# Gate matrices of an expert layer: from one-hot products on TensorE to indirect DMAs that add into DRAM, and one rounding moved from VectorE to ScalarE

## What is computed

```python
def one_block(xb):                                   # 128 tokens
    q = (xb @ w_query).reshape(PEER_BLOCK, PEER_HEADS, 2, PEER_HALF)
    s = jnp.einsum("thpd,hpkd->thpk", q, sub_keys)   # 8 heads, 2 halves, 128 keys
    s1, i1 = lax.top_k(s[:, :, 0], 16)
    s2, i2 = lax.top_k(s[:, :, 1], 16)
    cand = s1[..., :, None] + s2[..., None, :]
    sc, flat = lax.top_k(cand.reshape(..., 256), 16)
    e = i1[flat // 16] * 128 + i2[flat % 16]         # expert numbers
    g = jax.nn.softmax(sc, axis=-1)
    a = jax.nn.gelu(jnp.einsum("thkd,td->thk", u_emb[e], xb))
    return jnp.einsum("thk,thkd->td", g * a, v_emb[e])
```

## Time and profile before

| what | value |
|---|---|
| median of three runs | 3485.08 us (3483.61 to 3486.14) |
| span of the profiled execution | 3486.2 us |
| instructions | 47,324 |
| up stage, layer 0 / layer 1 | from 611.2 / from 2188.0 us, 746 us each |
| down stage, layer 0 / layer 1 | about 1357 to 1900 / 2934 to 3469 us |
| moved by DMA | 735 MB, 211 GB/s on average |

### The profile page before, as it was taken

The page is one execution under the profiler, slowest core; times in us unless marked ns, Lnnn a source line. Parts: engine busy times, 40 slices in busy tenths (PEclk is TensorE's granted clock), DMA queues, the critical chain, the costliest instruction groups (busy, mean ns, idle before and its releaser), DMA issues.

```text
span 3486.2 us, 47324 instructions
## 1 busy us (share of the span) xinstructions
PE 3400.2 (98%) x18196; PEld 2951.7 (85%) x18196; DVE 2360.2 (68%) x4309; ACT 1221.5 (35%) x1635; POOL 1194.6 (34%) x746
## 2 busy tenths in 40 slices
PE   7999889999999999999999989999999999999998
PEld 3886578888888889999999768888888888999998
DVE  6777720994487724998997330895477723999997
ACT  3216633333455532222223333333355532222222
POOL 0000033454100002776772453454200002877761
PEclk9999989999999999999999999999999999999999
DMA  7771030344455556999995230344455555999995
GB/s 284 260 252 49 25 145 1 127 145 145 160 191 222 198 180 219 365 359 366 384 376 210 73 122 12 110 146 145 159 206 186 222 183 202 357 370 361 359 361 198
DMA packets 286132, 735.16 MB, mean 211 GB/s; under 512 B 33362, under 2 KB 116947, under 8 KB 266196
## 3 DMA queue, kind: packets, MB, share of 16 engines
q1 hardware_dynamic: 203988, 530.63, 43.1%
q0 software_dynamic: 45056, 134.38, 10.3%
q10 hardware_dynamic: 36864, 67.13, 5.0%
HBM read 612.48 MB, written 119.54 MB: 210 GB/s over the span
## 4 chain that ended last, share of the span: by engine, by line
PE 93%; POOL 2%; DVE 2%; DMA 1%; ACT 1%; issue 1%; SPq 0%; DVEq 0%; POOLq 0%; ACTq 0%
PE ps L1373 40%; PE ps L1411 28%; PE ps L1175 5%; PE ps L1326 5%; PE ps L1277 5%; PE ps L1386 3%; PE ps L1203 2%; PE ps L1235 1%; POOL picked L1496 1%; PE ps L1215 1%; PE ps L1318 1%; PE ps L1129 1%; PE ps L1089 0%; POOL ring_lo L1484 0%; DMA modall<-in_w_mod 0%
## 5 line engine op out<-in xcount | busy, mean ns | idle before, releaser
L1373 PE MATMUL ps<-xhi,Uhi 128*128 128x512 f32 x2048 | 807.5, 394 | 0.0
L1373 PE MATMUL ps<-xhi,Ulo 128*128 128x512 f32 x2048 | 798.4, 390 | 0.0
L1373 PE MATMUL ps<-xlo,Uhi 128*128 128x512 f32 x2048 | 796.6, 389 | 0.0
L1496 POOL DMA_INDIRECT picked<-act_scratch,aidx x256 | 381.9, 1492 | 985.0 <-DMA act_scratch<-act_st 907.6
L1411 PE MATMUL ps<-Hhi,Vhi 128*128 128x384 f32 x2048 | 687.3, 336 | 6.7 <-DVE Hlo L2003 6.7
L1411 PE MATMUL ps<-Hlo,Vhi 128*128 128x384 f32 x2048 | 685.9, 335 | 0.0
L1411 PE MATMUL ps<-Hhi,Vlo 128*128 128x384 f32 x2048 | 685.8, 335 | 0.0
L1027 ACT CAST Vhi<-Vraw 128x1024 fp32r<-128x1024 f32 x256 | 269.8, 1054 | 787.0 <-PE ps L1411 766.4
L986 ACT ACTIVATE act_st<-ps 128x512 f32<-128x512 f32 x256 | 153.1, 598 | 869.6 <-PE ps L1373 535.1
L1373 PEld LDWEIGHTS ps<-xhi,Ulo 128*128 128x128 f32 x2048 | 384.3, 188 | 82.2
L1373 PEld LDWEIGHTS ps<-xlo,Uhi 128*128 128x128 f32 x2048 | 384.9, 188 | 77.6
(11 more groups left out here) (283 smaller groups left out, 4547.1 us busy)
## 6 DMA issues: line engine op xcount, KB each, us to landing
Uraw<-in_UT SPq DMA_DIRECT2D x128, 1024.0 KB, 5.7
Vraw<-in_V SPq DMA_DIRECT2D x256, 512.0 KB, 5.7
act_scratch<-act_st ACTq DMA_DIRECT2D x256, 256.0 KB, 5.5
G_scratch<-G_st SPq DMA_DIRECT2D x24, 2048.0 KB, 8.2
act<-act_scratch SPq DMA_DIRECT2D x256, 192.0 KB, 6.0
Gin<-G_scratch SPq DMA_DIRECT2D x192, 256.0 KB
modw<-in_w_mod SPq DMA_DIRECT2D x80, 512.0 KB, 4.8
ring<-in_query SPq DMA_DIRECT2D x8, 2048.0 KB, 8.0
```

The lines of the kernel that those rows point to most:

```text
L1373: mm = nc.tensor.matmul(up_bank(m), w, x[:, k, :], start=(k == 0 and j == 0), stop=(k == KT - 1 and j == 2))
L1496: nc.gpsimd.indirect_dma_start(picked[:, :, :].rearrange("p h k -> p (h k)")[:, p:p + 1], None, act_dram[layer].rearrange("m p (t o) -> (m ...
```

## The change

In place of the transposes, one-hot matrices, products, evictions and stores of G, POOL adds the weights one by one into a G in DRAM that was zeroed before: for each of the 384 pairs (token tile r = 1 to 3, head, place k) an indirect DMA of 128 floats with 128 offsets and `compute_op=ALU.add`. The offsets are computed at the end of `picks`. `PUTS` gives the order of the 24 groups of 16; a group waits until the group before of the same token tile has landed, since heads can hit the same element. G is now laid out as a tile of experts by 384 tokens, and the down stage loads it tile by tile, 192 KB each, four ahead.

The zeroes are written by SP from a zeroed strip in SBUF: 16 DMAs of 1.5 MB for layer 0 behind the second bias table, 16 for layer 1 beside tiles 41 to 71 of layer 0's up stage. POOL's subtractions end at tile 12; DVE does those of tiles 13 to 54 between the steps of `picks` (14 points for each of the token tiles that come second to fourth) and the rest behind them. The token tiles are routed in the order 1, 2, 3, 0. In the down stage ACT rounds H, ahead of the rounding of V two tiles on, where DVE did. The third `gate_in` chunk is loaded right behind the first two.

```diff
...
-HOTS_AT = 56
-REST_AT = HOTS_AT + 1
-EXP_AT = {13: 0, 25: 1, 37: 2, 49: 3}
-TURN_AT = {40: 1, 51: 2, 53: 3}
+ROUTE = (1, 2, 3, 0)
+REST_AT = 13
+POINTS = 14
+EXP_AT = {11: 0, 26: 1, 40: 2, 54: 3}
+WEIGHTS_AT = 56
+PUTS = ((0, 0), (0, 1), (0, 2), (1, 0), (0, 3), (1, 1), (0, 4), (2, 0), (1, 2), (0, 5), (2, 1), (1, 3),
+        (0, 6), (2, 2), (1, 4), (0, 7), (2, 3), (1, 5), (2, 4), (1, 6), (2, 5), (1, 7), (2, 6), (2, 7))
+NZ = 3 * P // 2
+ZROWS = 16
+ZERO_AT = 40
+NZERO = NE * TD // (P * ZROWS * NZ)
 LEAD = 112
 NPK = PH * TOPK
...
-        G_dram = nc.dram_tensor("G_scratch", (DEPTH, NCHT, P, NKEY, CHT), F32, kind="Internal").ap()
+        G_dram = [nc.dram_tensor(f"G_scratch{layer}", (NT, P, TD), F32, kind="Internal").ap()
+                  for layer in range(DEPTH)]
...
                 load_chunk(n)
+            def zero_gates(layer, n):
+                flat = G_dram[layer].rearrange("m p t -> (m p t)").rearrange("(p n z) -> p n z", p=P, z=NZ)
+                sp.dma_start(flat[:, n * ZROWS:(n + 1) * ZROWS, :],
+                             zeros[:, :].unsqueeze(1).to_broadcast([P, ZROWS, NZ])).then_inc(G_zeroed, 16)
...
                     sp.wait_ge(bias_used, h - 1)
                 sp.dma_start(btab[h % 2][:, :, :, :], a["btab"][2 * h:2 * h + 2].rearrange("h p s k -> p h s k")
                              ).then_inc(bias_in[h % 2], 16)
+                if h == 1:
+                    sp.wait_ge(zeros_ready, 1)
+                    for n in range(NZERO):
+                        zero_gates(0, n)
...
-            def load_gates(layer, q, c0, c1):
-                if q >= 2:
-                    sp.wait_ge(H_ready, layer * NT + (q - 1) * NGRP)
-                elif q == 1:
+            def load_gates(layer, m):
+                if m >= 4:
+                    sp.wait_ge(H_ready, layer * NT + m - 3)
+                elif m >= 2:
                     sp.wait_ge(up_mm, (layer + 1) * NT)
-                sp.dma_start(Gin[q % 2][:, c0:c1, :, :],
-                             G_dram[layer, c0:c1, :, q * NGRP:(q + 1) * NGRP, :].rearrange("c p j t -> p c j t")
-                             ).then_inc(G_in[q % 2], 16)
+                sp.dma_start(Gin[m % 4][:, :], G_dram[layer][m]).then_inc(G_in[m % 4], 16)
...
                     if m % 2 == 0 and 2 <= m < NT - 4:
                         load_U(m // 2 + 2)
-                    if m >= 1:
-                        for b in batches_after(m - 1):
-                            if (b + 1) * TOK % CHT == 0:
-                                store_gates(b * TOK // CHT)
+                    if layer == 0 and ZERO_AT <= m < ZERO_AT + 2 * NZERO and m % 2 == 1:
+                        zero_gates(1, (m - ZERO_AT) // 2)
                     if m == LEAD:
                         load_V(layer, 0)
                         load_V(layer, 1)
                         load_act(layer, 0)
-                for n in range(2):
-                    sp.wait_ge(G_stored[n], 16 * (layer + 1) * NCHT // 2)
-                for c in range(0, NCHT, GPIECE):
-                    load_gates(layer, 0, c, c + GPIECE)
+                for r in range(1, TT):
+                    sp.wait_ge(G_put[r], 16 * NPK * (layer + 1))
+                load_gates(layer, 0)
+                load_gates(layer, 1)
...
+                load_gates(layer, 2)
+                load_gates(layer, 3)
...
                         load_V(layer, m + NVRAW)
                     if m + 4 < NT:
                         load_act(layer, m + 4)
-                    if m % NGRP < NCHT // GPIECE and m // NGRP + 1 < NT // NGRP:
-                        c = m % NGRP * GPIECE
-                        load_gates(layer, m // NGRP + 1, c, c + GPIECE)
-                    if layer == 0 and 64 <= m < 64 + RING - 1:
+                        load_gates(layer, m + 4)
+                    if layer == 0 and 64 <= m < 64 + RING:
                         load_chunk(W_GIN + m - 64)
-                    if layer == 0 and m == NT - 4:
-                        sp.wait_ge(H_ready, NT - NGRP)
-                        load_chunk(W_GIN + RING - 1)
...
+            def round_H(layer, m):
+                act_e.wait_ge(H_step, layer * NT + m + 1)
+                if m >= 3:
+                    act_e.wait_ge(dn_mm, layer * (NT - 1) + m - 2)
+                nc.scalar.copy(Hhi[m % 3][:, :], Hf[m % 2][:, :]).then_inc(H_hi, 1)
             def peer_dense(layer):
                 for m in range(NT):
-                    i = layer * NT + m
+                    round_H(layer, m)
                     if m + 2 < NT:
                         split_V(layer, m + 2)
...
                 for m in range(NT):
                     up(m)
-                    if m in TURN_AT:
-                        turn_picks(TURN_AT[m])
-                    for b in batches_after(m):
-                        gate_weights(b)
...
                                             ALU.subtract).then_inc(U_split, 1)
+            def put_gates(layer):
+                pool.wait_ge(G_zeroed, 16 * NZERO * (layer + 1))
+                for order, h in PUTS:
+                    r = ROUTE[order]
+                    if h == 0:
+                        pool.wait_ge(pick_ready, layer * TT + order + 1)
+                    at_least(pool, G_put[r], 16 * (layer * NPK + h * TOPK))
+                    for k in range(TOPK):
+                        nc.gpsimd.indirect_dma_start(
+                            G_dram[layer].rearrange("m p (t o) -> (m p t) o", o=1),
+                            bass.IndirectOffsetOnAxis(ap=gidx[r][:, h * TOPK + k:h * TOPK + k + 1], axis=0),
+                            pick[r][:, 3, h, k:k + 1], None, compute_op=ALU.add).then_inc(G_put[r], 16)
...
             peer_rests(0)
+            put_gates(0)
             peer_rows(0)
...
+                def picks(order):
+                    r = ROUTE[order]
                     chosen = pick[r]
+                    def between(point):
+                        if order >= 1 and point is not None:
+                            rest_of_U(REST_AT + (order - 1) * POINTS + point)
...
                         for i in rows:
                             last = nc.vector.max_index(ids(i)[:, 8:16], vals(i)[:, 8:16], src(i))
                         step(last)
+                        between(points[4])
                     top16(range(HP), lambda i: topv[:, i // 2, i % 2, :], lambda i: topi[:, i // 2, i % 2, :],
-                          lambda i: S[:, i, r, :])
+                          lambda i: S[:, i, r, :], (0, 1, 2, 3, 4))
+                    if order >= 1:
+                        weights(order - 1)
...
                     step(last)
+                    between(5)
...
-                          lambda i: cand[:, 0, i, :])
+                          lambda i: cand[:, 0, i, :], (None, 6, None, 7, 8))
...
                     step(nc.vector.tensor_tensor(rank[:, 1, :, :], candi[:, :, :], rank[:, 1, :, :], ALU.subtract))
+                    between(9)
...
                     for half, keys in enumerate((key1[:, :, :], chosen[:, 2, :, :])):
                                                      ALU.is_equal))
                         step(nc.vector.tensor_tensor(eq[:, :, :, :], eq[:, :, :, :],
                                                      topi[:, :, half, :].unsqueeze(2).to_broadcast(shape), ALU.mult))
+                        between(10 + 2 * half)
                         step(nc.vector.tensor_reduce(keys, eq[:, :, :, :], AX, ALU.add))
+                        between(11 + 2 * half)
                     nc.vector.tensor_tensor(chosen[:, 3, :, :], candv[:, :, :],
...
+                    step(nc.vector.scalar_tensor_tensor(out=key1[:, :, :], in0=key1[:, :, :], scalar=float(NKEY),
+                                                        in1=chosen[:, 2, :, :], op0=ALU.mult, op1=ALU.add))
+                    if r > 0:
+                        nc.vector.tensor_scalar(gidx[r][:, :].rearrange("p (h k) -> p h k", h=PH), key1[:, :, :],
+                                                float(TD), row_no[:, r - 1:r], ALU.mult, ALU.add)
...
+                for r in range(1, TT - 1):
+                    if layer == 0:
+                        nc.vector.tensor_scalar(row_no[:, r:r + 1], row_no[:, 0:1], float(r * P), None, ALU.add)
+                for order in range(TT):
+                    picks(order)
+                for m in range(REST_AT + (TT - 1) * POINTS, NT):
+                    if m == WEIGHTS_AT:
+                        weights(TT - 1)
                     rest_of_U(m)
...
                 def gated(m):
-                    i = layer * NT + m
-                    q = m // NGRP
                     dve.wait_ge(act_in[m % 4], 16 * (layer * NT // 4 + m // 4 + 1))
-                    dve.wait_ge(G_in[q % 2], 16 * (NCHT // GPIECE) * (layer * NT // NGRP // 2 + q // 2 + 1))
-                    nc.vector.tensor_tensor(Hf[m % 2][:, :].rearrange("p (c t) -> p c t", t=CHT),
```

(11 more changed lines are left out.)

196 lines of the change are left out of this document (31 added, 165 removed).

## The result

The change makes the kernel slower: 3714.8 us (3700.4 to 3716.6), 1.0652 times the time before, 95% interval 1.0632 to 1.0673. The profiled execution spans 3711.7 us where that of before spans 3486.2. The forecast was 3393, and its range ended at 3620.

What follows compares the result with a forecast made beforehand. The prediction took PE's instruction stream, busy 98% of the span, as the bound. From a span of 3486.2 us it took 99 saved, plus 2 and 5, giving 3394.2, on the median 3393; own range 3375 to 3420, with rivals up to 3620.

Steps and rivals of the forecast that it cites:

- What leaves PE: Up stage: without gate matmuls and transposes it takes 696.7 us instead of 746.1, saving 49.5 us a layer, 99 in all.
- (d): Layer 1's zeroing beside tiles 41 to 71 of layer 0: gelu waits for stores, 0 to 6 us, taken as 2.
- The start and the collisions: POOL, up stage: puts start near 696; waiting for DVE instructions adds 0.24 us a put during routing, 0.11 after.
- The price of a put: POOL, up stage: a put costs 0.94 us like a gather, plus gap and collisions, so puts end at 1257, hidden.
- c: Mean cost of a put with its gap: forecast 1.39 us; PE waits beyond 1.526, and the sign turns at 1.63.
- puts dearer than gathers: Rival, POOL in the up stage: at 1.79 us a put with gap 3610 us, at 2.22 3940; chance 0.32.
- The premise behind the sum: Up stage: the saving holds only if the puts keep up with 5.44 us a tile and end by 1308.
- (a): Up stage: forty-four subtractions a layer move from POOL to DVE, with about 8.5 us of play; price 0.
- (b): Down stage: H rounded by ACT instead of DVE, ready some 2.1 us into a 4.16 us tile; price 0.
- (c): Layer 0's zeroing, issued in attention behind the second bias load, replaces G stores; price 0, at worst 10 us.
- (e): Tile-wise gate loads and third gate_in chunk behind the other two at tiles 64 to 66: 0 to 8 us, taken as 5.
- The act stores as the bound: Rival, up stage: every act store lands in 5.8 us and sets the tile, 3485 us at worst; chance 0.08.

Runs made afterwards that it cites:

- plain puts: The changed kernel with plain writes in place of the adds: 4223.9 us in one execution, beside 3504.9 for the kernel before.
- the gathers in their place: The changed kernel with its 768 indirect adds turned into reads from G into SBUF at the same offsets: 4192.3 us, ratio 1.198.
- the spaced ones: The changed kernel without the add, a POOL memset of 256 floats behind each put: 3490.6 us, ratio 0.9977; with 88 floats 3427.2 us.

## Why the prediction was wrong, point by point

**What leaves PE: right.** Forecast 696.7 us for an up stage, measured 702.1 and 696.6. The missing 5.5 is (d).

**The start and the collisions: right.** The first put was forecast for 696 and came at 697.9. The gap before a put is the 0.30 us of the gathers. The collisions, computed as 0.24 us a put during routing and 0.11 after it, were 0.20 (mean 1.744 up to 900 us, less 1.547) and 0.12 to 0.10 (means 1.666 and 1.645 until 1300). A single put shows the rule. POOL's timeline:

```profile
1002.56 2.26 POOL L1439 DMA_INDIRECT G_scratch<-pick,gidx  x1 [0.30 <-issue]
1005.12 1.55 POOL L1439 DMA_INDIRECT G_scratch<-pick,gidx  x1 [0.30 <-issue]
```

and DVE's:

```profile
1002.17 1.23 DVE L1760 TENSOR_TENSOR Ulo<-Uraw,Uhi 128x1024 fp32r<-128x1024 f32 x1 [3.19 <-ACT Uhi L940]
```

At 1002.56 the subtraction had 0.84 us to go, and the put took 0.71 more than its quiet 1.55: the remainder less 0.13, as for the gathers of the earlier trace rows. With PE and VectorE at rest (1320 to 1440) the mean is 1.548. The landings were priced too high: I took 7 us for each of three waits, and they are 1.8, 5.4 and 1.7 us long.

**The price of a put: the step that failed.** I took 0.94 us "because it is the same instruction with the same offsets". It was 1.55. By the prediction's own formula the rest follows: puts ending at 1459.2 make c = (1459.2 - 722) / 384 = 1.92, PE waits 384 x (1.92 - 1.526) = 151, and 3393 + 2 x (151 + 7.5) = 3710 where 3715 was measured. (This c is read from the end of the puts, so it tests the sum behind it and not the price. From the rows a put costs 1.654 + 0.305 = 1.96 in the mean, and the cheaper landings make up the difference.) The rival "puts dearer than gathers" thus describes what happened, in place and size; of its reason, a second read to describe, the runs show only that the add is what costs and that it comes with 144 packets in place of 32. Two errors made it the second choice. I read the price's independence of bytes as an argument that it would not depend on the operation either, which no row showed. And under an unknown whose bounds lay 0.98 us apart, a forecast that needed it to be within 0.13 us of the lower one had 0.48, while three quarters of the interval, above 1.18 us, was on the slow side. The top of the range was cut at c = 1.80, inside those bounds, and the result lay above it.

The Trainium skill, "DMA: Bandwidth & Descriptors", section "SDMA does more than copy", says that an add combines two streams; that pointed to the side on which the price fell. It gives no time, and the 1.8 us that I drew from it was too much: the run with the add left out puts the add at 0.59 us, on top of 0.96.

**The premise behind the sum: also wrong, unseen.** The sum let puts run at 1.24 us and up without asking what the DMA queues do with that. The plain puts and the gathers in their place show a loss of 370 to 400 us a layer from it, and the spaced ones none at 1.57. The rows of before could not show this: their gathers come in a burst of 24, which in that trace does no harm, or are paced by DVE. Since it is not shown that the chip of the result would have stalled, this is a risk that the prediction did not see, and not a second cause of its miss.

**(a) Subtractions on DVE: right in layer 1**, whose up stage of 696.6 leaves no room for a wait; in layer 0 see (d). **(b) Rounding on ScalarE: right for the changed kernel, in part by luck.** I named PE's tile as the cover and left out that the cast ahead of the rounding also waits for V's load, and H's rounding with it. In the changed kernel's trace those loads come in time (274 and 275 matmuls in the table above); where they don't, the rounding on ScalarE costs something, 3 to 13 us for both layers of the kernel before. **(c) Zeroes for layer 0: right.** The up stage starts at 610.6 us where it started at 610.9, and PE is busy 39.89 us of 300 to 340 as before, beside 372 GB/s. **(d) Zeroes for layer 1: size inside the range, mechanism not.** 2 us forecast, 5.5 measured (702.1 against 696.6), inside the 0 to 6. But 4.9 of it falls on two tiles, at 910 to 926 us, and not on 16 pairs. There the gelu waits 5.06 us for a store, the last exponential of the routing stands behind it on ScalarE, VectorE waits for that with the weights, and the next subtraction, for which PE waits, comes behind them:

```profile
916.43 0.29 DVE L1863 TENSOR_REDUCE zsum<-pick 128x8 f32<-128x128 f32 x1 [10.13 <-ACT pick L977]
```

Layer 1, without zeroes beside it, loses nothing at this place. **(e) The third chunk: right.** 5 us forecast with 8 as the most; taking it back is worth 6.6. Layer 0's down stage as a whole came out 4.6 us longer.

**The act stores as the bound: did not happen**; gelu waits for a store 48 times in 834 to 1226 us (205.9 us in all), and the up stage of layer 1 still stands at 5.44 us a tile with all puts running.

## What to carry over

A margin is worth what the widest unknown above it allows: where 384 instructions share 51 us, an unmeasured operation of the same form must be priced from both ends and the odds taken from where the turning point lies between them. Indirect DMAs hide behind PE as long as their number times their cadence fits, so move the share that fits (two token tiles of three here) and leave the rest where it was. Keep POOL's indirect DMAs some 1.6 us or more from each other where other loads must land beside them: a pause of 0.33 us was enough here. And compare a trace with one of the same sitting: the kernel before moved by up to 24 us between sittings, more than most of the edits of the down stage are worth.

## What the runs showed that I had not expected

- The add changes the packets as well. Page, third part, queue of POOL's DMAs (packets, MB, share), changed kernel, then plain puts:

```profile
q0 software_dynamic: 155648, 134.82, 17.9%
```

```profile
q0 software_dynamic: 69632, 134.82, 9.2%
```

  The difference is 86,016 = 768 x 112: a put with the add leaves 144 packets, one without it 32. Whether the 0.59 us of POOL time are spent on those was not tried.
- At one DMA of 128 offsets per 1.25 us from POOL, PE, ScalarE and SP's loads come to a near stop (18 to 21 us of PE work in 100) with DMA engines 11% busy, and with 30 GB/s moved; at 1.57 us there is no trace of it.
- At 1.85 us for a put with its gap, or more, and 146 GB/s in all, the adds cost the other queues nothing that PE sees in layer 1 (a window of that stage, columns as in the earlier trace rows):

```profile
2482.00:2982.00 500.00, 500.00 (x2207) 414.09 (x2206) 174.35 (x334) 147.17 (x190) 424.38 (x249) 1.00 0.62 146
```
